# Attention of a hybrid layer: probabilities divided before their transposes, values kept stationary over four heads, a rounded mask product, and values projected like the other tiles

## What is computed

```python
z = h @ w_in   # [pool 512 | q 512 | k 128 | v 128 | gate_pool 1024 | gate_attn 1024]
# window_attention: chunks of 64 tokens, each sees itself and the chunk before
scores = einsum('bcqhgd,bckhd->bchgqk', qc, kb) / sqrt(64)     # 8 query heads, 2 key/value heads
scores = where(valid, scores, -1e30)
probs = softmax(concatenate([scores, sink]))[..., :-1]          # a sink per head in the denominator
y_attn = einsum('bchgqk,bckhd->bcqhgd', probs, vb) @ w_branch_attn
merged = sigmoid(gate_pool) * (pool_mixer(p) @ w_branch_pool) + sigmoid(gate_attn) * y_attn
x = x + merged @ w_out
```

## Time and profile before

| | |
|---|---|
| time, median of 3 runs | 3030.55 us (3023.52 to 3033.89) |
| the profiled execution | 3019.19 us, span 3017.4 us |
| mean granted clock of TensorE | 0.972 of full |
| busy, share of the span | TensorE 94%, its weight load 82%, DVE 77%, GpSimd 70%, ScalarE 31% |
| DMA | 717.92 MB, mean 238 GB/s |

### The profile page before, as it was taken

How to read it: one execution, slowest core, us unless ns; L and a number is a source line. 1 busy time by engine, 2 the same in 40 slices (tenths; PEclk the granted TensorE clock), 3 DMA queues, 4 the chain that set the end, 5 groups by cost and what they waited for, 6 DMA issues and landing times.

```text
span 3017.4 us, 40171 instructions
## 1 busy us (share of the span) xinstructions
PE 2844.6 (94%) x15235; PEld 2477.6 (82%) x15235; DVE 2336.3 (77%) x4348; ACT 937.1 (31%) x1356; POOL 2124.3 (70%) x1552
## 2 busy tenths in 40 slices
PE   7999898999899799899999998999999989999996
PEld 6678777677689688889998997899899979989995
DVE  1332298345499899588999999898899979889998
ACT  4232433232332399322222222222222222222221
POOL 4324576338568799778887886888688868878883
PEclk9899999899899899999999999999999999999998
DMA  3112412112322377989998997999899979989996
GB/s 140 43 63 91 168 64 70 42 50 98 112 87 94 120 238 237 332 310 330 347 349 315 342 336 289 335 342 341 311 343 336 346 266 339 348 311 341 335 337 219
DMA packets 267584, 717.92 MB, mean 238 GB/s; under 512 B 20864, under 2 KB 104064, under 8 KB 267392
## 3 DMA queue, kind: packets, MB, share of 16 engines
q0 software_dynamic: 110912, 403.75, 35.8%
q1 hardware_dynamic: 156480, 311.61, 30.6%
HBM read 657.86 MB, written 57.41 MB: 237 GB/s over the span
## 4 chain that ended last, share of the span: by engine, by line
PE 34%; DVE 8%; POOL 7%; DMA 6%; issue 3%; ACT 1%; DVEq 0%; SPq 0%; ACTq 0%
PE abank L1530 6%; PE abank L1532 6%; PE abank L1531 6%; PE ybank L1546 6%; PE ybank L1547 5%; PE ybank L1548 5%; POOL up L1475 3%; DVE acc L1684 3%; DMA up<-in_down,e_idx 3%; POOL tdown_lo L1482 2%; DMA up<-in_up,e_idx 2%; DVE up L1672 2%; DVE e_y L1731 1%; POOL tup_lo L1486 1%; DMA w<-all_pre 1%
## 5 line engine op out<-in xcount | busy, mean ns | idle before, releaser
L1530 PE MATMUL abank<-m_hT,tdown_hi 128*128 128x384 f32 (+1 forms) x1856 | 576.4, 311 | 15.0 <-ACT w L1588 9.0
L817 POOL TENSOR_TENSOR m_wlo<-m_raw,m_whi 128x1024 fp32r<-128x1024 f32 x128 | 309.5, 2425 | 379.9 <-ACT m_whi L622 376.7
L1532 PE MATMUL abank<-m_hT,tdown_lo 128*128 128x384 f32 (+1 forms) x1856 | 575.9, 310 | 0.0
L1531 PE MATMUL abank<-m_hlo,tdown_hi 128*128 128x384 f32 (+1 forms) x1856 | 574.9, 310 | 0.0
L1546 PE MATMUL ybank<-tup_hi,w_hi 128*128 128x512 f32 x1280 | 509.1, 398 | 45.5 <-DVE e_y L1731 32.7
L1684 DVE SCALAR_TENSOR_TENSOR acc<-up,e_act,acc 128x1024 f32<-128x1024 f32 x381 | 489.7, 1285 | 65.9 <-DMA up<-in_up,e_idx 43.4
L1672 DVE CUSTOM_DVE_ANT_0 up<-up,acc 128x1024 f32<-128x1024 f32 x384 | 457.0, 1215 | 97.8 <-DMA up<-in_down,e_idx 95.2
L1547 PE MATMUL ybank<-tup_lo,w_hi 128*128 128x512 f32 x1280 | 506.2, 396 | 0.0
L1548 PE MATMUL ybank<-tup_hi,w_lo 128*128 128x512 f32 x1280 | 504.2, 394 | 0.0
L1475 POOL DMA_INDIRECT up<-in_up,e_idx x384 | 396.9, 1033 | 106.0 <-issue 92.4
L1475 POOL DMA_INDIRECT up<-in_down,e_idx x384 | 399.1, 1039 | 99.3 <-issue 88.9
(11 more groups left out here) (226 smaller groups left out, 4714.6 us busy)
## 6 DMA issues: line engine op xcount, KB each, us to landing
e_tup<-in_up SPq DMA_DIRECT2D x128, 512.0 KB
m_raw<-in_tiles SPq DMA_DIRECT2D x116, 512.0 KB, 3.3
e_tdown<-in_downT SPq DMA_DIRECT2D x116, 512.0 KB
gates<-all_table SPq DMA_DIRECT2D x64, 640.0 KB
all_table<-t_out SPq DMA_DIRECT2D x9, 4096.0 KB, 14.7
m_raw<-in_downT SPq DMA_DIRECT2D x12, 512.0 KB, 3.7
up<-in_down,e_idx POOLq DMA_INDIRECT x384
up<-in_up,e_idx POOLq DMA_INDIRECT x384
```

The source lines that it names most:

```text
L1530: nc.tensor.matmul(out, tdown_hi[:, q, at], h2T_hi[:, k, a:b], start=k == 0, stop=False)
L1531: nc.tensor.matmul(out, tdown_hi[:, q, at], h2T_lo[:, a:b, at], start=False, stop=False)
L1532: ins = nc.tensor.matmul(out, tdown_lo[:, q, at], h2T_hi[:, k, a:b], start=False, stop=k == KD - 1)
```

## The change

Four edits, and what they carry with them:

- the value tile goes through `project`, comes out with tokens along the columns, is copied to the free `q4[:, 3]`, and a new job `vT` transposes it (4 matmuls) behind `q 0`;
- the mask and its rows become a tile of their own, loaded by one DMA and rounded once by ScalarE to fp32r, so the mask matmul has rounded operands;
- a new function `shares` divides the probabilities in SBUF, four heads at a time, ahead of their transposes; the transposes wait for it (`pr_ready`), and the sinks' exponential stands ahead of the heads';
- the `pT` banks are filled by key half instead of by head, and `pv` is four matmuls with 64 columns of values stationary and four heads (512 columns) moving. The result has tokens along the columns already, so the job `yaT` and the tile `ya` are gone. The rows of `w_branch_attn` are permuted on the host to match.

```diff
@@ mixer_jobs
     for j in range(4):
         jobs += [("q", j)]
+        if j == 0:
+            jobs += [("vT",)]
...
-        jobs += [EARLY[t], ("pv", t), ("grp", t), ("yaT", t)]
+        jobs += [EARLY[t], ("pv", t), ("grp", t)]
@@ sync
             for n in range(RING):
                 load_tile(n)
+            sp.dma_start(mask_in_f32[:], io["mask"]).then_inc(mask_in, 16)
@@ tensor
-                out = begin("v")
-                w_hi, w_lo = weights("v")
-                for t in range(TT):
-                    for k in range(KD):
-                        at = slice(k * P, (k + 1) * P)
-                        ins = term(out[:, t * P:(t + 1) * P], hT[:, k, t], hlo[:, t, at], w_hi[:, at], w_lo[:, at],
-                                   k == 0, k == KD - 1)
-                ins.then_inc(job_full, 1)
+                project(("v",), ("v",))
...
                     project(("q", j), ("q", j))
+                    if j == 0:
+                        pe.wait_ge(vT_kept, g + 1)
+                        turn(("vT",), [q4[:, 3, t * P:(t + 1) * P] for t in range(TT)])
...
-                        nc.tensor.matmul(out[:, 0:2 * WK], const[:, C_ROWS:C_ROWS + P], mask, start=True, stop=False)
+                        nc.tensor.matmul(out[:, 0:2 * WK], mask[:, 0:P], unseen, start=True, stop=False)
...
                     for i in range(4):
-                        pe.wait_ge(exp_ready, g * 9 * TT + 9 * t + 2 * i + 2)
-                        turn(("pT", t, i), [pr[:, 2 * i + e // 2, (e % 2) * P:(e % 2 + 1) * P] for e in range(4)])
+                        kv, e = i // 2, i % 2
+                        pe.wait_ge(pr_ready, 2 * (g * TT + t) + kv + 1)
+                        turn(("pT", t, i), [pr[:, 4 * kv + j, e * P:(e + 1) * P] for j in range(4)])
...
-                    for hd in range(NH):
-                        kv, at = slice(hd // 4 * HD, (hd // 4 + 1) * HD), slice(hd * HD, (hd + 1) * HD)
-                        nc.tensor.matmul(out[:, at], prT[:, 2 * hd], v[:, t, kv], start=True, stop=False)
-                        ins = nc.tensor.matmul(out[:, at], prT[:, 2 * hd + 1], v[:, t + 1, kv],
-                                               start=False, stop=True)
+                    for kv in range(2):
+                        for e in range(2):
+                            ins = nc.tensor.matmul(out[kv * HD:(kv + 1) * HD], v[:, t + e, kv * HD:(kv + 1) * HD],
+                                                   prT[:, 8 * kv + 4 * e:8 * kv + 4 * e + 4].rearrange("p j c -> p (j c)"),
+                                                   start=e == 0, stop=e == 1)
...
-                    pe.wait_ge(ya_ready, g * TT + t + 1)
-                    turn(("yaT", t), [ya[:, j * P:(j + 1) * P] for j in range(4)])
@@ vector
+                def shares(t):
+                    for kv in range(2):
+                        of = slice(4 * kv, 4 * kv + 4)
+                        dve.wait_ge(exp_ready, g * 9 * TT + 9 * t + 4 * kv + 5)
+                        link(nc.vector.tensor_tensor(den[:, of], rs[t % 2][:, of], es[t % 2][:, of], ALU.add))
+                        link(nc.vector.reciprocal(den[:, of], den[:, of]))
+                        nc.vector.tensor_tensor(pr[:, of, CH:], pr[:, of, CH:], den[:, of].unsqueeze(2).to_broadcast([P, 4, WK]),
+                                                ALU.mult).then_inc(pr_ready, 1)
 
                 maxima(0)
                 for t in range(TT):
+                    shares(t)
...
-                    if t:
-                        ya_low(t - 1)
                     if t + 1 < TT:
                         maxima(t + 1)
-                    dve.wait_ge(exp_ready, g * 9 * TT + 9 * t + 9)
-                    link(nc.vector.tensor_tensor(den, rs[t % 2], es[t % 2], ALU.add))
-                    link(nc.vector.reciprocal(den, den))
-                    wait_job(dve, g, "pv", t)
-                    nc.vector.tensor_tensor(ya[:].rearrange("p (a c) -> p a c", a=NH),
-                                            bank("pv", t)[:].rearrange("p (a c) -> p a c", a=NH),
-                                            den.unsqueeze(2).to_broadcast([P, NH, HD]), ALU.mult).then_inc(ya_ready, 1)
+                    ya_low(t)
```

More of the change, by code:

```diff
@@ L211, in mixer @@
         h32 = place("h32", [P, KD, LEAD], F32, at_pr + 4096)
-        at_ya = here()
-        ya = place("ya", [P, NH * HD])
+        mask = place("mask", [P, NMASK], F32R)
         at_yaT = here()
@@ L270, in mixer @@
         prT_ready = sem("prT_ready")
-        ya_ready = sem("ya_ready")
+        mask_in, mask_ready = sem("mask_in"), sem("mask_ready")
+        vT_kept = sem("vT_kept")
+        pr_ready = sem("pr_ready")
         yaT_ready, yaT_low = sem("yaT_ready"), sem("yaT_low")
@@ L502, in scores @@
                             pe.wait_ge(zeroed, 1)
-                    mask = const[:, C_MASK:C_MASK + 2 * WK] if t == 0 and g == 0 else const[:, C_MASK + 2 * WK:C_MASK + 4 * WK]
+                            pe.wait_ge(mask_ready, 1)
+                    unseen = mask[:, P:P + 2 * WK] if t == 0 and g == 0 else mask[:, P + 2 * WK:]
                     for i in range(4):
                         out = begin("sc", t, i)
-                        nc.tensor.matmul(out[:, 0:2 * WK], const[:, C_ROWS:C_ROWS + P], mask, start=True, stop=False)
+                        nc.tensor.matmul(out[:, 0:2 * WK], mask[:, 0:P], unseen, start=True, stop=False)
                         for e in range(2):
@@ L666, in _ @@
             tile_high(RING)
+            act.wait_ge(mask_in, 16)
+            nc.scalar.activation(mask[:], mask_in_f32[:], ACT.Copy).then_inc(mask_ready, 1)
             act.wait_ge(zeroed, 1)
@@ L683, in _ @@
                 wait_job(act, g, "v")
-                nc.scalar.activation(v[:, 1:1 + TT].rearrange("p t c -> p (t c)"), bank("v")[:], ACT.Copy).then_inc(v_ready, 1)
+                nc.scalar.activation(q4[:, 3], bank("v")[:], ACT.Copy).then_inc(vT_kept, 1)
                 after("v")
@@ L688, in _ @@
                     after("q", j)
+                    if j == 0:
+                        wait_job(act, g, "vT")
+                        nc.scalar.activation(v[:, 1:1 + TT].rearrange("p t c -> p (t c)"), bank("vT")[:],
+                                             ACT.Copy).then_inc(v_ready, 1)
                 def expon(t):
@@ L710, in _ @@
                     after(*EARLY[t])
+                    wait_job(act, g, "pv", t)
+                    nc.scalar.activation(yaT[:, :, t * P:(t + 1) * P],
+                                         bank("pv", t)[:].rearrange("p (j c) -> p j c", j=4), ACT.Copy).then_inc(yaT_ready, 1)
                     wait_job(act, g, "grp", t)
@@ L881, in _ @@
                 pool.wait_ge(rope_in, 16 * (g + 1))
+                pool.wait_ge(mask_ready, 1)
                 pool_mean(g, 0)
@@ L1790, in tiles_of @@
     pool, q, k, v, gp, ga = np.split(w_in, np.cumsum([POOL_W, NH * HD, P, P, D]), axis=1)
+    heads = w_branch_attn.reshape(2, 4, HD, D).transpose(1, 0, 2, 3).reshape(NH * HD, D)
     q = q.reshape(D, 2, 4, HD).transpose(0, 2, 1, 3).reshape(D, NH * HD)
     tiles = {"p": columns(pool), "k": columns(k), "v": columns(v), "q": columns(q), "gp": columns(gp), "ga": columns(ga),
-             "b": np.concatenate([columns(w_branch_pool), columns(w_branch_attn)], axis=2),
+             "b": np.concatenate([columns(w_branch_pool), columns(heads)], axis=2),
              "out": w_out.reshape(KD, P, D), "pq": columns(w_peer_q)}
@@ L1806, in constants @@
             c[base + (d + half) % rot, C_PERM + base + d] = 1
-    c[0, C_ROWS:C_ROWS + CH] = 1
-    c[1, C_ROWS + CH:C_ROWS + P] = 1
-    mask = c[:, C_MASK:C_MASK + 4 * WK].reshape(P, 4, WK)
-    mask[0, :, P:] = -1e30
-    mask[1, :, 0:CH] = -1e30
-    mask[0, 0:2, 0:CH] = -1e30
-    c[:, C_IOTA:C_IOTA + P] = np.arange(P)
+    c[:, C_IOTA:C_IOTA + P] = np.arange(P)
+    m = np.zeros((P, NMASK), np.float32)
+    m[0, 0:CH] = 1
+    m[1, CH:P] = 1
+    unseen = m[:, P:].reshape(P, 4, WK)
+    unseen[0, :, P:] = -1e30
+    unseen[1, :, 0:CH] = -1e30
+    unseen[0, 0:2, 0:CH] = -1e30
     pos = np.arange(T, dtype=np.float32)
@@ L1828, in constants @@
         r[0, :, R_CNT + j * PAD:R_CNT + (j + 1) * PAD] = w / np.minimum(np.arange(PAD) + 1, w)
-    return c, r
+    return c, m, r
 def arrays_of(x, g_mix, w_in, w_pool_grp, pool_scale, attn_sinks, w_branch_pool, w_branch_attn, w_out, g_ffn,
               w_peer_q, peer_keys_1, peer_keys_2, expert_down, expert_up, g_final):
-    c, r = constants()
+    c, m, r = constants()
     vecs = np.concatenate([g_mix[0].reshape(KD, P).T, g_ffn[0].reshape(KD, P).T, pool_scale[0].reshape(NPOOL, P).T,
@@ L1837, in arrays_of @@
     return {
-        "x": x.reshape(NG, TT, P, D), "const": c, "rope": r, "vecs": vecs,
+        "x": x.reshape(NG, TT, P, D), "const": c, "mask": m, "rope": r, "vecs": vecs,
         "tiles": tiles_of(w_in[0], w_branch_pool[0], w_branch_attn[0], w_out[0], w_peer_q[0]),
```

29 lines of the change are left out of this document (13 added, 16 removed).

## The result

The changed kernel takes 3033.60 us (median of 20 runs, 3025.49 to 3043.11), the kernel before 3023.51 us beside it (20 runs, 3016.66 to 3033.89): ratio 1.0032, interval [1.0024, 1.004], so +10 us. The profiled execution has a span of 3029.4 us, against 3017.4 before.

What follows compares the result with a forecast made beforehand. TensorE's gapless job list in the attention stage was taken as the bound. Terms without the clock summed to -6.3 us, the clock added +18.6, giving +12.3 us on the median 3030.55: 3043 us, range 3020 to 3060.

Steps and rivals of the forecast that it cites:

- values like other tiles: Value projection: 24 products of 512 columns replace 96 narrow ones, four transposes added; 4.7 us gained, twice, -9.3 us.
- rounded mask: Mask products ahead of the scores: rounded operands shorten them, 0.51 us each at full clock, twice that at half; -20.4 us.
- values stationary over four heads: Probabilities times values: four unrounded products of 512 columns take 3.64 us instead of 3.51, eight times; +1.0 us.
- division ahead of the first transposes: Block 0 of each group: transposes wait for sum, reciprocal and multiply, next mask product at 112.8 against 110.6; +4.4 us.
- wait behind the pooled product: Blocks 1 to 3: TensorE idle 3.1 us until DVE divides the next block; +3.0 us, six times, +18.0 us.
- clock: Granted clock falls to 0.50 behind 8 in 10 of the new idle gaps, plus 1 us per first block; +18.6 us.
- The bound below, -6.3: Lower bound for values stationary over four heads: the two middle products of each four overlap wholly, 7.3 us gone in all.
- Rival 3: Middle products of the four overlap by 7.3 us and the clock holds: -13.6 us, 3017 us; chance 0.08.
- rival 1: The new gaps come behind the pooled product but the clock does not fall: -6.3 us, 3024 us; chance 0.20.
- the row of the forecast: Block 0 before the change: scores stayed at clock 0.50 and the transposes of 107 to 111 brought it back.

Runs made afterwards that it cites:

- v_alone: Kernel before with only the value edit (value tile projected like the others, turned by four transposes): 3018.31 us, ratio 0.9988 to the kernel before.
- v_mask: Kernel before with the value edit and the rounded mask, old order of attention and division kept: 3007.52 us, ratio 0.9952 to the kernel before.
- its repetition: v_mask run once more unchanged, with its own profile: 2999.58 us, ratio 0.9938 to the kernel before.
- mask_unrounded: Changed kernel with its mask tile kept as plain float32 instead of rounded: 3031.84 us, ratio 1.0027 to the kernel before.
- filled: Changed kernel with 11 spare rounded products per block on TensorE during the wait ahead of the transposes, blocks 1 to 3: 3012.53 us, ratio 0.9966 to before.
- extra_pair: Changed kernel with the two value products of the first half of the heads made twice per block: 3056.36 us, ratio 1.0106 to the kernel before.
- early_shares: Changed kernel with VectorE dividing the next block right behind its maxima, ahead of two small subtractions: 2992.85 us, ratio 0.9901 to the kernel before.
- gate_tile_first: Changed kernel with early_shares' VectorE order and the early gate tile projected ahead of the probabilities' transposes: 2979.41 us, ratio 0.9856 to the kernel before.

## Why the number came out near, and which step was wrong

The forecast was 3043 us (3020 to 3060) and slower by 12.3 us; measured were 3033.6 us and +10.1. Of the 9.4 us between the two times, 7.0 are the base: the three runs shown had a median of 3030.55, twenty have 3023.51. That +10.1 lies so near to +12.3 is luck. Every term of the forecast lies ahead of the mark, and there the two profiles of the changed kernel are only 3.7 and 1.6 us behind the one of before, less than a mark scatters. One term was 14 us wrong, and without that error the forecast would have been -2 us. The rest of the measured +10.1 came up in the experts' part, of which the forecast said nothing. Term by term:

| step | forecast | measured | from |
|---|---|---|---|
| values like other tiles | -9.3 | -7.2 | marks, v_alone to before |
| rounded mask | -20.4 | -20.2 | marks, v_mask and its repetition (-22.6, -17.8) to v_alone |
| values stationary over four heads | +1.0 | **-13.1** | 1.87 instead of 3.51 us, eight times |
| division ahead of the first transposes | +4.4 | +4.7 | score product to next mask product, 16.00 (88.09 to 104.09) against 13.63 in v_mask, twice |
| wait behind the pooled product | +18.0 | +17.5 | pooled to mask product, 6.18 in mask_unrounded (full clock) against 3.26, six times |
| clock | +18.6 | +15 to +21 | filled against the changed kernel, marks and medians |

**The step that failed** is the one at the values stationary over four heads: "as half-height score products follow one another without overlap", "I take the +1.0". The products of a block take 1.87 us and not 3.64, and the term is -13.1 us. The rows of another shape did not carry over. The two score products of a pair both read the half of the rows that their one key head has, which I take for the reason that they did not overlap (no run tests it); two of these four write the one column half and two the other, and extra_pair shows that all of them pair up. The bound below, -6.3, was too high as well, since I let only the two middle ones overlap. Rival 3, whose mechanism this was, did not end on the faster side, because the clock did fall.

**What held.** The value tile is 9.5 us shorter by its rows in two groups (5.58 us and 0.35 for the four transposes, for 10.67); its mark shows 7.2, for the reason given at v_alone. The wait was forecast at 3.1 us and is 2.84 with 0.19 behind it; its releaser is DVE's multiply, forecast at 0.95 us and measured at 0.96; DVE does there, in this order, what the forecast listed. early_shares shows that the order alone makes it. The clock fell at six places of six instead of 8 in 10; it was back with the transposes or just behind them at four and stayed low through the scores at two, where I had taken half. filled shows it as a cost of its own, and rival 1 (the clock holds) falls with it.

**What was right in size and incomplete in its mechanism** is the clock. I had it follow from the wait alone. mask_unrounded has that wait and hardly a fall. So rounding and clock are not two terms that add up: of v_mask's gain by the mask nothing is left once the wait is there.

**What stays open.** With the measured terms the sum is -3.6 us at the mark (clock at 14.7), and 3.7 and 1.6 were measured; 2.7 of that is the longer half clock at block 0 (10.2 us more, 4.8 of it waiting), the rest is less than the 4.8 us by which two profiles of one kernel differ. So that the stage itself became slower is not shown; that it did not become some 30 us faster, as v_mask and early_shares did, is. And of the +10.1 us of the medians only about 2.7 stand at the mark. The other 7 lie in the experts' part: 1999.2 and 2002.3 us in two profiles of the changed kernel, 1990.9 in before's one, which is the shortest of all twelve profiles. Some of it is clock too: behind the mark 91 and 84 us were at half clock in these two, 80 in before's. Over whole executions, one less the granted clock, times the span, comes to 116 us in the 29 of the changed kernel and 86 in the 52 of before beside the experiments, 30 us more; by the profiles 23 of these stand ahead of the mark. In v_mask's long experts' part 99 us were at half clock and in its repetition's 80, which makes 10 of the 19 us between them. What moves the clock there no run separates.

## What to carry to other kernels

When a step is moved ahead of something that TensorE waits for, write down what its engine does just ahead of it in program order: the same division put the mark 34 us later behind two small subtractions, which wait for TensorE and ScalarE, than in front of them. Put a dense tile between a chain over two other engines and the products that wait for it; with the division in its early place that took 1.4% off the kernel before (gate_tile_first, 0.9856). And count an edit that shortens products next to a wait together with the clock: the same edit was worth 20 us without the wait and nothing with it.

## What the runs showed of the hardware that was not expected

- Float32 products on 64 columns with 512 moving ones take 0.86 us each in one column half (two loads, 0.43 us apart) and 1.87 us for four over both halves, although both of the first half stand ahead of both of the second in TensorE's list. So a product of the second half started ahead of one of the first that stands before it.
- The transposes do not bring the clock back reliably. In the ten profiles that have them right behind the first scores, full clock came back between some 0.1 us ahead of the next mask product's start and 2.5 us behind it in 12 of 20 first blocks (14 to 24 us at half clock in all), and only behind all the next scores in 8 (27 to 31 us). Two executions of the changed kernel had it in different groups. In the forecast I had one row for it and set it against the Trainium skill (TensorE: Matmul & The Clock Gate, Part 4: PE-mode transpose), by which transposes do not raise the clock: over twenty places the traces agree with that rule in 8. In filled's group 0 they do not: full clock was back at about 103.1, with nothing but the wait of 4.45 us and the transposes from 100.08 on behind the scores, ahead of the next mask product at 103.24. In the other 11, the row of the forecast among them (111.7 against 110.64), the next scores had begun by then, and the transposes' part in it is not shown. A dense gate tile brought it back each time in gate_tile_first.
- A wait of 2.84 us was followed by a fall at 18 of 18 places with the rounded mask (two profiles of the changed kernel and extra_pair) and at 1 of 6 with the unrounded one.
